# Attention over heads of 64 on one Trainium2 core: score and value products of two heads interleaved on TensorE

## The reference, cut to what matters

```python
# even layer, first half: 8 heads of 64 (at 512 tokens every earlier block is selected)
s = jnp.einsum('bhqd,bhkd->bhqk', qc, k_own) * scale + b_own        # causal, bias by distance
p = jax.nn.softmax(jnp.concatenate([s_own, s_sel], -1), -1)
o = p @ v
# even layer, second half: 4 heads, each of two 64-wide score maps that share a value of 128
s = jnp.einsum('bhcqd,bhckd->bhcqk', qb, k) * scale                 # c = 0, 1
p = jax.nn.softmax(jnp.where(dist >= 0, s + bias[None, :, None], NEG), axis=-1)
a = p[:, :, 0] - lam * p[:, :, 1]
o = jnp.einsum('bhqk,bhkd->bhqd', a, v)                             # then an rmsnorm per head
# odd layer, first half: 8 heads of 64, dilated windows, written here as one causal bias per head
```

## Time and profile before

| | |
|---|---|
| median of 3 runs | 3023.8 us (3023.45 to 3033.6) |
| the profiled execution | 3033.55 us, its span 3031.7 us |
| mean granted TensorE clock | 0.978 |
| PE busy | 2895.5 us of the span (96%) |
| DVE, ACT, POOL busy | 45%, 31%, 19% |
| PE on the chain that ended last | 88% |
| even stage of 8 heads | about 1727 to 1868 us of the span |
| stage of the double heads | about 1868 to 1979 us |
| odd stage of 8 heads | about 2389 to 2528 us |

### The profile page before, as it was taken

How to read it: one execution, slowest core, us unless ns; L and a number is a source line. 1 busy time by engine, 2 the same in 40 slices (tenths; PEclk the granted TensorE clock), 3 DMA queues, 4 the chain that set the end, 5 groups by cost and what they waited for, 6 DMA issues and landing times.

```text
span 3031.7 us, 32274 instructions
## 1 busy us (share of the span) xinstructions
PE 2895.5 (96%) x13454; PEld 2313.7 (76%) x13454; DVE 1379.3 (45%) x2023; ACT 953.9 (31%) x1276; POOL 569.2 (19%) x441
## 2 busy tenths in 40 slices
PE   7979989999998999999999999899999999999998
PEld 4757677788887878877888877678888865688886
DVE  5463463657534333333222454645345454544353
ACT  3353343321223322333222332432222333332222
POOL 3444351110112211221101100012112100012021
PEclk9989989999999999999999999999999999999999
DMA  6311112446422222222632321122232321122321
GB/s 236 107 42 63 62 43 97 154 163 232 163 89 100 74 87 84 87 70 87 169 116 80 108 80 65 53 81 91 87 109 75 111 63 51 59 100 76 120 80 66
DMA packets 49808, 294.29 MB, mean 97 GB/s; under 512 B 6345, under 2 KB 6473, under 8 KB 23808
## 3 DMA queue, kind: packets, MB, share of 16 engines
q1 hardware_dynamic: 43632, 274.48, 25.7%
q0 software_dynamic: 4736, 15.43, 1.9%
q10 hardware_dynamic: 1296, 2.32, 0.2%
HBM read 283.56 MB, written 8.65 MB: 96 GB/s over the span
## 4 chain that ended last, share of the span: by engine, by line
PE 88%; DVE 6%; ACT 4%; issue 1%; DMA 0%; POOL 0%; SPq 0%; DVEq 0%; ACTq 0%
PE ps L218 87%; ACT F L1135 1%; DVE wlo L211 1%; PE ps L1159 1%; ACT whi L200 0%; DVE F L2068 0%; DVE F L356 0%; DVE hl L360 0%; DMA F<-in_ada 0%; ACT hh L369 0%; DVE F L1126 0%; DVE E L2629 0%; ACT F L1176 0%; DVE F L1171 0%; DVE ada L399 0%
## 5 line engine op out<-in xcount | busy, mean ns | idle before, releaser
L218 PE MATMUL ps<-hh,whi 128*128 128x512 f32 x2088 | 833.4, 399 | 34.4 <-DVE hl L360 14.5
L218 PE MATMUL ps<-hh,wlo 128*128 128x512 f32 x2088 | 821.2, 393 | 0.0
L218 PE MATMUL ps<-hl,whi 128*128 128x512 f32 x2088 | 821.2, 393 | 0.0
L211 DVE TENSOR_TENSOR wlo<-raw,whi 128x2048 fp32r<-128x2048 f32 (+2 forms) x235 | 496.2, 2111 | 562.4 <-ACT whi L200 557.4
L218 PE MATMUL ps<-R,whi 128*128 128x512 f32 x2080 | 650.8, 392 | 7.8 <-DVE wlo L211 2.8
L200 ACT ACTIVATE whi<-raw 128x2048 fp32r<-128x2048 f32 (+2 forms) x235 | 409.6, 1743 | 727.5 <-PE ps L218 727.4
L218 PEld LDWEIGHTS ps<-hh,whi 128*128 128x128 f32 x2088 | 397.2, 190 | 133.8 <-issue 27.0
L218 PEld LDWEIGHTS ps<-R,whi 128*128 128x128 f32 x2080 | 391.1, 188 | 95.1 <-issue 6.9
L218 PEld LDWEIGHTS ps<-hl,whi 128*128 128x128 f32 x2088 | 397.0, 190 | 84.7
L218 PEld LDWEIGHTS ps<-hh,wlo 128*128 128x128 f32 x2088 | 397.3, 190 | 82.8 <-issue 2.4
L218 PE MATMUL ps<-R,wlo 128*128 128x512 f32 x1040 | 405.2, 390 | 0.0
(11 more groups left out here) (318 smaller groups left out, 2566.2 us busy)
## 6 DMA issues: line engine op xcount, KB each, us to landing
F<-in_ada SPq DMA_DIRECT2D x32, 1024.0 KB, 4.8
raw<-in_fs0in SPq DMA_DIRECT2D x22, 1024.0 KB, 5.6
raw<-in_fs1in SPq DMA_DIRECT2D x22, 1024.0 KB, 4.8
raw<-in_fc0in SPq DMA_DIRECT2D x22, 1024.0 KB, 4.8
raw<-in_fc1in SPq DMA_DIRECT2D x22, 1024.0 KB, 4.8
Rf<-in_ada0h SPq DMA_DIRECT2D x24, 512.0 KB, 3.5
raw<-in_fs0out SPq DMA_DIRECT2D x16, 704.0 KB, 4.7
raw<-in_fs1out SPq DMA_DIRECT2D x16, 704.0 KB, 4.1
```

Of the source, the lines that this page charges most:

```text
L211: e.tensor_tensor(m.wlo[n % 2][:, 0:size], m.raw[m.slot[n]][:, 0:size], m.whi[n % 2][:, 0:size].bitcast(F32), SUB).then_inc(*s.up("wlo", n))
L218: return e.matmul(out, l, r, start=start, stop=stop, skip_group_check=True)
```

## The change

Heads are taken in pairs. The score products of a pair alternate between partitions 0 to 63 and 64 to 127, and its value products between output partitions 0 to 63 and 64 to 127. To have both heads' scores in PSUM at once there is a table of places for each of the two (`PAIR`), which now uses banks 5 and 6 too, those of the transposes. The second head of a pair has a buffer of its own for its turned weights (in `E`). The double heads take the same pair function for their two maps; their values stay as they are. DVE and ACT take both heads' scores before the first reciprocal.

```diff
 PLACE = {3: (2, 0), 2: (3, 0), 0: (3, 384), 1: (4, 0)}
+PAIR = [{3: (2, 0), 2: (4, 0), 0: (4, 384), 1: (6, 0)}, {3: (3, 0), 2: (5, 0), 0: (5, 384), 1: (6, 256)}]
...
+    def scored(self, c):
+
+        return (*self.key, 0) if c == 2 else (*self.second, 1) if c == 1 else (*self.key, c)
...
+def pe_pair_scores(e, s, m, groups, a):
+
+
+    for c, n in ((3, 0), (3, 1), (1, 0), (2, 1), (2, 0), (0, 1), (0, 0), (1, 1)):
+        if (c, n) == (1, 1):
+            s.wait_ge("score", *groups[0].key, 1)
+        g, rows = groups[n], slice(64 * n, 64 * n + 64)
+        b, o = g.place[c]
+        q, k = a[rows, c * P:(c + 1) * P], a[rows, T:T + (c + 1) * P]
+        mm(e, m.ps[b][:, o:o + (c + 1) * P], q, k).then_inc(*s.up("score", *g.key, c))
...
+def pe_pair_values(e, s, m, groups, values, out):
+    for g in groups:
+        for c in range(4):
+            s.wait_ge("pt_act" if c % 2 else "pt_dve", *g.key, c)
+    for i in range(4):
+        for n, g in enumerate(groups):
+            t = mm(e, out[64 * n:64 * n + 64, i * P:], values[n](i), pt_of(m, g)[:, i, i * P:], i == 0, i == 3)
+    t.then_inc(*s.up("pv", *groups[1].key))
...
-    yield from (("qk", 0), ("v", 0), ("v", 1), ("a", 0), ("a", 1))
-    for h in range(8):
-        if h % 2 == 0 and h < 6:
-            yield "qk", h // 2 + 1
-        if h == 6:
-            yield "next", 0
-        yield "t", h
-        if h < 6:
-            yield "a", h + 2
-        yield "pv", h
+    yield from (("qk", 0), ("v", 0), ("v", 1), ("a", 0))
+    for p in range(4):
+        yield ("qk", p + 1) if p < 3 else ("next", 0)
+        yield "t", p
+        if p < 3:
+            yield "a", p + 1
+        yield "pv", p
...
+                s.wait_ge("smax", st, 2 * i - 1, 1)
+                s.wait_ge("pt_act", st, 2 * i - 1, 1)
+                s.wait_ge("pt_dve", st, 2 * i - 1, 0)
+            pe_pair_scores(e, s, m, h64_pair(st, i), h64_qk(m, i))
...
-            dve_scores(e, s, m, g, m.f(A_BIAS + T * (i % 2)))
-            dve_recip(e, s, m, g)
-            dve_weights(e, s, m, g)
+            for n, g in enumerate(h64_pair(st, i)):
+                s.wait_ge(f"bias{n}", st, 2 * i + n)
+                dve_scores(e, s, m, g, m.f(A_BIAS + T * n))
+            for g in h64_pair(st, i):
+                dve_recip(e, s, m, g)
+                dve_weights(e, s, m, g)
...
+                s.wait_ge("smax", "diff", i - 1, 1, 1)
+                s.wait_ge("pt_act", "diff", i - 1, 0, 1)
+                s.wait_ge("pt_dve", "diff", i - 1, 0, 0)
+            pe_pair_scores(e, s, m, [diff_group(i, n) for n in range(2)], m.f(A_QK, 2 * T))
...
             for g in (g0, g1):
                 dve_scores(e, s, m, g, m.f(A_BIAS))
+            for g in (g0, g1):
                 dve_recip(e, s, m, g)
```

More of the change, by code:

```diff
@@ L1090, with __init__ @@
 class Group:
-    def __init__(self, key, slot, stat, before, slot_before, pt_before):
-        self.key, self.slot, self.stat = key, slot, stat
+    def __init__(self, key, slot, stat, before, slot_before, pt_before, place=PLACE, pt=0, second=None, turn_before=None):
+        self.key, self.slot, self.stat, self.place, self.pt, self.second = key, slot, stat, place, pt, second or key
         self.before, self.slot_before, self.pt_before = before, slot_before, pt_before
+        self.turn_before = turn_before or pt_before
     def p(self, m, c=None):
@@ L1107, in pe_scores @@
     for c in (3, 2, 0, 1):
-        b, o = PLACE[c]
+        b, o = g.place[c]
         if g.before and c != 0:
@@ L1123, in dve_scores @@
     for c in (3, 2, 0, 1):
-        b, o = PLACE[c]
-        s.wait_ge("score", *g.key, c if c != 2 else 0)
+        b, o = g.place[c]
+        s.wait_ge("score", *g.scored(c))
         e.tensor_tensor_reduce(out=g.p(m, c), in0=m.ps[b][:, o:o + (c + 1) * P], in1=bias[:, 384 - 128 * c:512], scale=1.0, scalar=-3.0e38,
@@ L1152, in pe_turn @@
     for c in (3, 2, 1, 0):
-        if c >= 2 and g.pt_before:
-            s.wait_ge("pt_act" if c == 3 else "pt_dve", *g.pt_before, c - 2)
+        if c >= 2 and g.turn_before:
+            s.wait_ge("pt_act" if c == 3 else "pt_dve", *g.turn_before, c - 2)
         elif c < 2:
@@ L1211, in h64_group, with h64_pair @@
     key = lambda i: (st, i) if i >= 0 else None
-    return Group((st, h), h % 3, h % 4, key(h - 1), key(h - 3), key(h - 1))
+    last = key(h - 1 if h % 2 == 0 else h - 2)
+    return Group((st, h), h % 3, h % 4, None, key(h - 3), last, PAIR[h % 2], h % 2, key(h | 1), key(h - 1))
+def h64_pair(st, p):
+    return [h64_group(st, 2 * p), h64_group(st, 2 * p + 1)]
 def h64_qk(m, p):
@@ L1254, in pe_h64 @@
         elif what == "a":
-            g, (p, hh) = h64_group(st, i), divmod(i, 2)
-            s.wait_ge("qk", st, p, 1)
+            s.wait_ge("qk", st, i, 1)
             if i == 0:
                 s.wait_ge("rcol", prev)
-                s.wait_ge(V_BY[1], st, 1, 3)
-            a, rows = h64_qk(m, p), slice(64 * hh, 64 * hh + 64)
-            pe_scores(e, s, m, g, [(a[rows, 0:T], a[rows, T:2 * T])])
+                for t in range(4):
+                    s.wait_ge(V_BY[t % 2], st, 1, t)
+            else:
+                s.wait_ge("smax", st, 2 * i - 1, 1)
+                s.wait_ge("pt_act", st, 2 * i - 1, 1)
+                s.wait_ge("pt_dve", st, 2 * i - 1, 0)
+            pe_pair_scores(e, s, m, h64_pair(st, i), h64_qk(m, i))
         elif what == "t":
-            for t in range(4) if i == 0 else ():
-                s.wait_ge(V_BY[t % 2], st, 1, t)
-            pe_turn(e, s, m, h64_group(st, i))
-        else:
[L1267 to L1270, removed]
+            for g in h64_pair(st, i):
+                pe_turn(e, s, m, g)
+        else:
+            if i:
+                s.wait_ge("o_lo_dve", st, i - 1)
+            pe_pair_values(e, s, m, h64_pair(st, i), [lambda c, h=h: values[:, c, 64 * h:64 * h + 64] for h in (2 * i, 2 * i + 1)], m.ps[7])
 def act_h64(e, s, m, st):
@@ L1381, in diff_group @@
     key = lambda i, k: ("diff", i, k) if i >= 0 else None
-    before = key(h, 0) if n else (key(h - 1, 1) or ("even", 7))
     if n:
@@ L1386, in diff_group @@
         slot, last = h % 2, key(h - 2, 0)
-    return Group(("diff", h, n), slot, (2 * h + n) % 4, before, last, key(h - 1, 0) or ("even", 7))
+    return Group(("diff", h, n), slot, (2 * h + n) % 4, None, last, key(h - 1, 0) or ("even", 7), PAIR[n], 0, key(h, 1))
 def diff_order():
@@ L1421, in pe_diff @@
             if i == 0:
-                s.wait_ge(V_BY[1], "diff", 1, 3)
-            a = m.f(A_QK, 2 * T)
-            for n in range(2):
-                rows = slice(64 * n, 64 * n + 64)
-                pe_scores(e, s, m, diff_group(i, n), [(a[rows, 0:T], a[rows, T:2 * T])])
+                for t in range(4):
+                    s.wait_ge(V_BY[t % 2], "diff", 1, t)
+            else:
+                s.wait_ge("smax", "diff", i - 1, 1, 1)
+                s.wait_ge("pt_act", "diff", i - 1, 0, 1)
+                s.wait_ge("pt_dve", "diff", i - 1, 0, 0)
+            pe_pair_scores(e, s, m, [diff_group(i, n) for n in range(2)], m.f(A_QK, 2 * T))
         elif what == "t":
```

28 lines of the change are left out of this document (14 added, 14 removed).

## The result

| | before | after |
|---|---|---|
| median | 3027.2 us (4 runs, 3023.45 to 3033.6) | 2994.66 us (4 runs, 2993.81 to 2999.46) |
| the profiled execution | 3033.55 us, span 3031.7 us | 2999.46 us, span 2997.7 us |
| mean granted clock | 0.978 | 0.976 |

The ratio of after to before is 0.9894, 95% interval 0.9871 to 0.9916. The change makes the kernel faster by about 1.1%, more than this kernel's measurement needs to be told from nothing. The forecast was 3001.5 us and its range 2996 to 3018 us, so the time lies 1.3 us under the lower end: the direction was forecast rightly, the gain too small.

The account below looks back on a forecast made before the run. TensorE, busy 96% of the span, was taken as the bound. Savings of 24.9 us, less 1.0 for double heads and 1.6 for clock, gave 22.3 us off the median 3023.8: 3001.5 us, range 2996 to 3018 us.

Parts of the forecast that it names:

- What bounds the kernel: Whole kernel: TensorE, busy 96% of the span, bounds it; DVE or ACT time counts only where TensorE waits for it.
- The scores of a pair: Score products of two heads, alternating row halves: 3.30 us against 4.7 us, each record starting 0.107 us after the one before.
- the values: Value products of two heads, alternating column halves: 2.78 us against 4.6 us, with loads spaced 0.055 us.
- The turns: Transposes of two heads with their waits for copies out of banks 5 and 6: 4.50 us against 4.10 us.
- Pair, last pair, first scores: Stages of eight, first scores also in first double head: savings of 16.9, 4.1 and 3.9 us, together 24.9 us.
- Double heads: Double heads 0 to 2: DVE gets block 2 later, at 3.09 us, so 0.33 us lost each, 1.0 us together.
- The clock: The qk after double heads: longer TensorE waits before norm bring one more half-clock spell, costing 1.6 us.
- From profile to median: Whole time: the 22.3 us gain was subtracted from the median 3023.8 us, not the profiled 3033.55 us, giving 3001.5 us.
- rival 1: Value products: column halves do not overlap, values take 4.43 us a pair, 13.2 us more, 3014.7 us; chance 0.22.
- rival 2: Pairs' turns: four waits lower the clock, a 1.6 us spell in each of eight, 12.8 us lost, 3014 us; chance 0.12.
- Rival 3: Scores and values: alternation gives no overlap (4.47 and 4.43 us) and the new waits stay, 3028.7 us; chance 0.06.
- The rule that was set aside: Products on array halves: the skill's about 4 ns per added tile, making the gain some 35 us; 0.1 us was used instead.

## Why the prediction was right or wrong

- **What bounds the kernel** held: time on TensorE counted in full, in the stages of eight heads to 0.1 us a window.
- **The scores of a pair**, 3.30 us, were 2.36, and **the values**, 2.78 us, were 2.30. This is the step that failed: "a record of the other half starts one load, 0.107 us, after the start of the record before it". Two things in it were wrong. The first is the price. I had read a cost of 0.1 us off the one change of half in the trace and charged it at each of seven changes (0.055 us for the values). The runs show it is paid once, at the first product of a run; the row at 1769.19 would have told me, since its step of 0.50 us has no change of half in it. The second is the order. By the rule B's first record comes behind A's second, as in the program, 0.53 us after A's first; it came 7 ns after A's first, and the series show a free half reaching four records ahead. Worked through again with this order and no price, the rule gives 2.87 us for the scores and 2.66 us for the values (an estimate from the record times of the prediction). So the price made 0.43 and 0.12 us of the error, and the order the other 0.51 and 0.36. The choice between the ends then went to the wrong one: for the values the lower bound named was 2.3 us, and measured were 2.30.
- **The turns** were right: 4.64 for 4.50 us, with the waits for the copies where they were put. That they were a price and not fixed was not seen: seven banks make them 2.27 us.
- **Pair, last pair, first scores**: 9.30 for 10.58, 6.90 for 7.33, 2.36 for 3.30 us. The sum of 24.9 us measured 24.6 + 5.0 + 6.8 = 36.4, which is 11.5 us more: 12.3 from that one step (nine scores, eight values), less 0.9 for the turns.
- **Double heads.** The mechanism was right (block 2 waits for product 0A, the square sits behind the exponentials, nothing of the products saved comes out), the size followed the same rule: block 2 came to DVE 2.42 us after the scores' start and not 3.09, so head 0 gained 0.24 us where 0.33 was to be lost; over three heads it is 0.6 us gained for 1.0 lost.
- **The clock**: one more spell, 1.6 us, was forecast; the windows show 2.4 + 0.56 = 3.0 us.
- **From profile to median.** Measured span difference is 34.0 us for 22.3; the medians differ by 32.5 (3027.2 less 2994.66). The forecast went from the median of 3023.8 us of three runs, which one more run moved up by 3.4. That, the clock, and the 1.5 us between spans and medians brought the time to within 1.3 us of the range though the sum was off by a third. So near a miss is luck.
- **The rivals.** Column halves overlap wholly, so rival 1 is out. The clock in the pairs' windows stayed at 1.00 with all four waits in them, so rival 2 is. Rival 3 is out too: it had a chain of alternating products take 4.47 and 4.43 us, and they took 2.36 and 2.30. Even with both products in series the kernel took 3019.55 us and not its 3028.7, because there A's last four records run beside B's.
- **The rule that was set aside.** The Trainium skill ("TensorE: Matmul & The Clock Gate", "Measured speedup vs the span model") has about 4 ns for each further tile of a pack, and by it the prediction had "some 35 us" for the gain. The first records on row and column halves started 6 to 7 ns apart, and the same terms measured 36.4 us. The rule agrees with the trace; my reading of the earlier trace rows does not. The same page of the Trainium skill ("The mechanism") lets a weight load overlap only where the row group differs, and has products start strictly in program order. The column halves share their rows, and their loads (1809.51 and 1809.52) and records start as close together as those of the row halves; and in the run with the values in series B's first record (1805.58) starts ahead of A's sixth (1805.79), which stands before it in the program. On both the measurement decides against the page.

The range could have held the time: its lower end was put at a gain of 28 us, though the text itself named 2.3 us for the values and a rule for 35 us. A bound that is worked out belongs in the range.

## What to carry to other kernels

Two streams of products on opposite halves of the array, rows or columns, cost as much as one here, and for fp32 they may come in blocks of two products; only longer runs on one half (four products, three) lost part of the overlap. Before a single row is made a rule, look for the same step where the suspected cause is absent. And once products get cheap, look at what stands between them: here the waits for copies and for ACT's square were worth as much again (2994.66 to 2963.01 us) as the change.

## What the runs showed of the hardware that I had not expected

- Records of a free half start ahead of program order, four records deep at most in every place tried (3.86 and 3.94 us in series, 2.36 in blocks of two, 3.21 in blocks of three, 2.30 alternating).
- A wait that is released early leaves this alone (3.93 us); a late one costs its delay once (4.35 us).
- The second record of the first product of a run comes 0.50 to 0.53 us after the first, for a record of 0.427 us (scores; 0.48 for values, as from 1809.51 to 1809.99). It does so with and without the other half running.
